# Late input products and the second short convolution placed around the first gathers, output products in quarters, row sums one slot at a time

## The reference, cut to what matters

```
z = rmsnorm(x) @ w_in                       # 19 column blocks of 128: groups A, B, C, D
A: conv31(glu) -> layernorm -> silu         # "conformer"
B: RWKV-7 time mixing, chunks of 64 tokens
C: gate_b * conv3(gate_c * hc)              # "short convolution"
D: trailing means over 2/4/8/16 positions
x = x + concat[A, B, C, D] @ w_out
q = rmsnorm(x) @ wq;  scores against 2 x 128 keys per head (8 heads)
top 16 of 16 x 16 sums -> 16 experts per token and head, gates = softmax
out = sum over experts of gate * gelu(u_e . x) * v_e;   x = x + out;  rmsnorm
```

## Time and profile before

| | us |
|---|---|
| median of 3 runs | 1668.51 |
| lowest, highest | 1665.66, 1673.72 |
| the profiled execution | 1671.36 |
| its span (first to last instruction) | 1669.6 |
| PE, DVE, ACT, POOL busy | 1220.8, 1236.3, 709.3, 916.7 |
| mean granted TensorE clock | 0.842 |
| DMA: bytes moved, mean rate | 605.42 MB, 363 GB/s |
| of it the gathers (queue 0) | 545.29 MB |

### The profile page before, as it was taken

How to read it: one execution, slowest core, us unless ns; L and a number is a source line. 1 busy time by engine, 2 the same in 40 slices (tenths; PEclk the granted TensorE clock), 3 DMA queues, 4 the chain that set the end, 5 groups by cost and what they waited for, 6 DMA issues and landing times.

```text
span 1669.6 us, 19415 instructions
## 1 busy us (share of the span) xinstructions
PE 1220.8 (73%) x5360; PEld 615.6 (37%) x5360; DVE 1236.3 (74%) x2935; ACT 709.3 (42%) x2021; POOL 916.7 (55%) x1135
## 2 busy tenths in 40 slices
PE   8998898766676877677886767675766676767564
PEld 6887756322233544332332323232322232323110
DVE  3878767788878887677778777777667776767775
ACT  3322223555454444344455654443444443434444
POOL 0364012557565766454566655565665576656662
PEclk9999999888797998788998778787878877767777
DMA  7321468999999999999999999999999999999996
GB/s 217 115 89 51 98 217 290 420 417 378 417 419 396 415 417 396 416 415 416 353 418 419 417 419 417 418 418 418 410 406 418 412 409 414 417 404 407 420 412 280
DMA packets 109308, 605.42 MB, mean 363 GB/s; under 512 B 22905, under 2 KB 25337, under 8 KB 42641
## 3 DMA queue, kind: packets, MB, share of 16 engines
q0 software_dynamic: 74880, 545.29, 79.8%
q1 hardware_dynamic: 34304, 58.89, 10.8%
q10 hardware_dynamic: 16, 0.02, 0.0%
HBM read 600.97 MB, written 3.19 MB: 362 GB/s over the span
## 4 chain that ended last, share of the span: by engine, by line
DMA 37%; PE 27%; DVE 16%; POOL 6%; issue 6%; ACT 4%; DVEq 3%; POOLq 0%; SPq 0%
DMA arena<-in_uv,arena 35%; PE ps L1011 11%; DVE arena L1979 8%; PE ps L612 5%; POOL arena L2233 4%; DVEq L1414 3%; PE ps L962 3%; DVE arena L1417 3%; POOL arena L2232 2%; PE ps L684 2%; DVE arena L1423 2%; PE ps L981 1%; ACT arena L1344 1%; PE ps L663 1%; ACT arena L1340 1%
## 5 line engine op out<-in xcount | busy, mean ns | idle before, releaser
L1011 PE MATMUL ps<-arena 128*64 128x512 f32 x2048 | 659.5, 779 | 368.5 <-ACT arena L1344 367.2
L1979 DVE CUSTOM_DVE_ANT_0 arena<-arena 128x1024 f32<-128x1024 f32 x520 | 640.8, 1234 | 292.6 <-DMA arena<-in_uv,arena 270.7
L2233 POOL DMA_INDIRECT arena<-in_uv,arena x520 | 617.8, 1188 | 87.2 <-POOL arena L2232 17.3
L2232 POOL TENSOR_TENSOR arena<-arena 1x1 f32<-1x1 f32 x520 | 216.7, 417 | 501.0 <-PE ps L1011 412.2
L1011 PEld LDWEIGHTS ps<-arena 128*64 128x64 f32 x2048 | 151.0, 164 | 754.3 <-ACT arena L1344 521.1
L1338 ACT ACTIVATE arena<-arena 128x1 f32<-128x1 f32 x520 | 105.1, 202 | 699.4 <-DVE arena L1979 697.1
L1344 ACT ACTIVATE arena<-arena 128x64 f32<-128x64 f32 (+1 forms) x520 | 181.4, 349 | 16.9
L1340 ACT ACTIVATE arena<-arena 128x1 f32<-128x1 f32 x520 | 153.2, 295 | 16.9
L1417 DVE TENSOR_TENSOR arena<-arena 128x512 f32<-128x512 f32 (+9 forms) x312 | 134.6, 432 | 21.6 <-ACT arena L1096 7.4
L612 PE MATMUL ps<-arena 128*128 128x264 f32 (+1 forms) x608 | 141.2, 386 | 0.3 <-DVE arena L1417 0.3
L962 PEld LDWEIGHTS ps<-arena 128*128 128x128 f32 x1024 | 126.9, 205 | 38.4 <-issue 37.3
...
## 6 DMA issues: line engine op xcount, KB each, us to landing
arena<-in_win SPq DMA_DIRECT2D x38, 512.0 KB, 3.4
...
arena<-in_wout SPq DMA_DIRECT2D x24, 512.0 KB, 4.9
arena<-in_uv,arena POOLq DMA_INDIRECT x520
arena<-in_xp SPq DMA_DIRECT2D x4, 512.0 KB, 6.6
out_yp<-arena SPq DMA_DIRECT2D x4, 512.0 KB
arena<-in_wqk SPq DMA_DIRECT2D x15, 128.0 KB
...
```

The source lines that it names most:

```text
L1011: last = mm(ps[64 * q:64 * q + 64, b + c, :], diag[:, (s + q) % 8, :], ring[:, SLOT_OF[TOPK * u + s + q], D + 512 * c:D + 512 * c + 512], ...
L1979: v.tensor_tensor_reduce(out=here, in0=here, in1=row, scale=1.0, scalar=0.0, op0=MUL, op1=ADD, accum_out=hsel[:, u % 2, s:s + 1]).then_inc ...
L2232: pool.tensor_tensor(carrier[:, 1:2], carrier[:, 0:1], carrier[:, 0:1], ALU.add).then_inc(S["carried"], 1)
L2233: pool.indirect_dma_start(out=ring[:, SLOT_OF[k], :], out_offset=None, in_=a["uv"][:, :], in_offset=bass.IndirectOffsetOnAxis(ap=idx[:, t, ...
```

## The change

- `SLOT_OF`, `FREE`, `FRESH`: slots 0 to 6 take seven free buffers, slots 7 to 13 reuse them, slot 14 takes the eighth and is the one that waits for all z copies. The weight ring moves below the band 1 input; slot 5 now waits until the weight ring has been used up.
- z blocks 31 to 37 leave the weight ring: they load into two buffers `zlate` from SP's `late_weights`, and PE runs one after the seventh tile 1 output block's product, one after `turned(1, ...)`, and one after each of the first five pairs of slots of unit 0. ACT copies them at the places shown. SP issues `late_weights(2)` to `(6)` before the first `next_keys`.
- `sums` handles one slot: the two column groups now hold the two halves of v, the two PSUM banks the even and the odd slot. `add_unit` adds four quarters of 64 x 512 in place of one 128 x 1024.
- `project_out` does four of eight blocks per call, at four ticks in place of two.
- Group C of band 1 moves from POOL (`short(1)`) to DVE (`short_second`), and DVE's taps, `conf_center`, `conf_scale`, `conf_swish` and the steps of `choose(1, ...)` are placed anew; the first keys are loaded three weight blocks earlier.

```
@@ -114,9 +114,9 @@
 RING = 8
-SLOT_OF = [0, 1, 2, 3, 4, 0, 1, 2, 3] + [(5, 6, 7, 4, 0, 1, 2, 3)[k % 8] for k in range(8 * 65)]
-FREE = (0, 1, 2, 3, 4, 9, 10, 11)
-FRESH = 9
+SLOT_OF = 2 * list(range(7)) + [(7, 0, 1, 2, 3, 4, 5, 6)[k % 8] for k in range(8 * 65)]
+FREE = (0, 1, 2, 3, 4, 5, 6, 14)
+FRESH = 14
@@ -136,7 +136,7 @@
...
 ZFRONT = 31
-Z_HIGH = 35
+Z_HIGH = 33
@@ -153,8 +153,7 @@
     return [("z", j) for j in range(lo, hi)]
-BLOCKS = z_blocks(0, ZFRONT) + out_blocks(0, 0, 2) + z_blocks(ZFRONT, ZFRONT + 1) + out_blocks(0, 2, 6) + z_blocks(ZFRONT + 1, ZFRONT + 2) \
-    + out_blocks(0, 6, 8) + out_blocks(1, 0, 5) + z_blocks(ZFRONT + 2, len(ZORDER))
+BLOCKS = z_blocks(0, ZFRONT) + out_blocks(0, 0, 8) + out_blocks(1, 0, 5)
@@ -295,9 +294,9 @@
...
         o_h = o_r + 3344 + 256
-        o_hb = o_ring + RING * ROW - 3 * KT * 128 - KT * GT
-        o_w = o_hb + KT * GT
-        assert o_w + 3 * KT * 128 == o_up and o_h + KT * GA <= o_hb and o_hb >= o_ring + 5 * ROW
+        o_hb = o_ring + RING * ROW - KT * GT
+        o_w = o_hb - 3 * KT * 128
+        assert o_h + KT * GA <= o_w and o_hb == o_ring + 7 * ROW and o_w >= o_ring + 5 * ROW
@@ -519,20 +521,29 @@
...
                 weights(n)
-                k = n - n_out - 8
+                k = n - n_out - 5
...
                     sp_.dma_start(wqk[:, 2048:2304], a["wqk"][0][:, 2048:2304]).then_inc(d_k12, 16)
-                elif k == 5:
-                    sp_.wait_ge(S["short_done"], 2)
-                    for i, j in enumerate(ASIDE):
-                        sp_.dma_start(w_aside[i], a["wout"][:, OUT_ORDER[j], :]).then_inc(d_aside, 16)
+            sp_.wait_ge(S["short_done"], 2)
+            for i, j in enumerate(ASIDE):
+                sp_.dma_start(w_aside[i], a["wout"][:, OUT_ORDER[j], :]).then_inc(d_aside, 16)
+
+            def late_weights(i):
+                if i >= 2:
+                    sp_.wait_ge(S["z_done"], ZFRONT + i - 1)
+                sp_.dma_start(zlate[i % 2].rearrange("p a b -> p (a b)"), a["win"][ZORDER[ZFRONT + i][0]]).then_inc(d_late[i % 2], 16)
+
             sp_.wait_ge(S["tails_done"], 3)
+            for i in range(2):
+                late_weights(i)
...
             sp_.dma_start(lora_b, a["lora"][:, :]).then_inc(d_lorab, 16)
+            for i in range(2, len(ZORDER) - ZFRONT):
+                late_weights(i)
             def next_keys(n):
@@ -601,15 +612,20 @@
...
                     i, g = ZORDER[j]
-                    n = BLOCK_OF[("z", j)]
                     lo, hi = BANDS[g]
-                    pe.wait_ge(d_w[n % 3], 16 * (n // 3 + 1))
+                    if j < ZFRONT:
+                        n = BLOCK_OF[("z", j)]
+                        pe.wait_ge(d_w[n % 3], 16 * (n // 3 + 1))
+                        w = wring[:, n % 3]
+                    else:
+                        pe.wait_ge(d_late[(j - ZFRONT) % 2], 16 * ((j - ZFRONT) // 2 + 1))
+                        w = zlate[(j - ZFRONT) % 2]
...
                     for k in range(KT):
-                        last = mm(ps[:, z_bank(j), 0:hi - lo], wring[:, n % 3, k, :], hT[g][:, k, :], start=(k == 0), stop=(k == KT - 1))
+                        last = mm(ps[:, z_bank(j), 0:hi - lo], w[:, k, :], hT[g][:, k, :], start=(k == 0), stop=(k == KT - 1))
@@ -657,11 +673,11 @@
...
                     last.then_inc(S["block_used" if j < KT - 1 else "out_mm"], 1)
-            def project_out(t, nh):
-                n, (_, y) = width(t), Y_ROWS[t]
-                for j in range(KT):
-                    last = mm(ps[0:n, 5 + nh, :], y[:, OUT_ORDER[j], :], w_blocks[j][:, 512 * nh:512 * nh + 512], start=(j == 0), stop=(j == KT - 1))
-                if nh:
+            def project_out(t, nh, part):
+                y = Y_ROWS[t][1]
+                for j in range(4 * part, 4 * part + 4):
+                    last = mm(ps[:, 5 + nh, :], y[:, OUT_ORDER[j], :], w_blocks[j][:, 512 * nh:512 * nh + 512], start=(j == 0), stop=(j == KT - 1))
+                if nh and part:
@@ -844,23 +860,22 @@
...
                 tiles = (2, 3, TILES)
-                def project(k, nh):
+                def project(k, nh, part):
                     t = tiles[k]
-                    if not nh:
+                    if not nh and not part:
...
                     if t < TILES:
-                        project_out(t, nh)
-                    else:
+                        project_out(t, nh, part)
+                    elif part:
...
                 for k in range(3):
-                    yield C_OUT + 7 * k
-                    project(k, 0)
-                    yield C_OUT + 7 * k + 4
-                    project(k, 1)
+                    for piece in range(4):
+                        yield C_OUT + 7 * k + (0, 2, 4, 5)[piece]
+                        project(k, piece // 2, piece % 2)
@@ -936,16 +951,13 @@
...
             first_out(0, 0, 2)
-            zcol()
...
             first_out(0, 2, 6)
-            zcol()
...
             first_out(1, 0, 1)
-            conf_mean(1)
@@ -1005,33 +1017,33 @@
             def sums(u, s):
                 b = 2 * (u % 2)
-                pe.wait_ge(S["diag_done"], TOPK * u + s + 2)
+                k = TOPK * u + s
+                pe.wait_ge(S["diag_done"], k + 1)
                 for c in range(2):
-                    for q in range(2):
-                        last = mm(ps[64 * q:64 * q + 64, b + c, :], diag[:, (s + q) % 8, :],
-                                  ring[:, SLOT_OF[TOPK * u + s + q], D + 512 * c:D + 512 * c + 512],
-                                  start=(s == 0 and u in FIRST_OF), stop=(s == TOPK - 2 and u in LAST_OF))
-                        if c:
-                            last.then_inc(S["slot_used"], 1)
-                for q in range(2):
-                    if u + LEAD < NU:
-                        prepare(u + LEAD, s + q)
-                    later.until(pace(TOPK * u + s + q + PE_AHEAD))
+                    last = mm(ps[64 * c:64 * c + 64, b + s % 2, :], diag[:, s % 8, :], ring[:, SLOT_OF[k], D + 512 * c:D + 512 * c + 512],
+                              start=(s < 2 and u in FIRST_OF), stop=(s >= TOPK - 2 and u in LAST_OF))
+                last.then_inc(S["slot_used"], 1)
+                if u + LEAD < NU:
+                    prepare(u + LEAD, s)
+                later.until(pace(k + PE_AHEAD))
             query(0)
+            score(0)
+            first_out(1, 1, 2)
+            conf_mean(1)
+            first_out(1, 2, 8)
+            zcol()
             conf_variance(1)
-            score(0)
-            first_out(1, 1, 8)
-            zcol(3)
...
             turned(1, 1)
+            zcol()
...
             pe.wait_ge(S["z_copied"], Z_HIGH)
-            sums(0, 0)
-            zcol()
-            sums(0, 2)
-            zcol()
+            for s in range(0, 10, 2):
+                sums(0, s)
+                sums(0, s + 1)
+                zcol()
...
             def unit(u):
@@ -1051,7 +1063,7 @@
...
                     return
-                for s in range(4 if u == 0 else 0, TOPK, 2):
+                for s in range(10 if u == 0 else 0, TOPK):
@@ -1286,9 +1298,7 @@
...
                 first.until(C_CH + 6 * c + 4)
-            zc()
             first.finish()
-            zc()
@@ -1325,7 +1335,6 @@
...
             queries(0)
-            conf_root(1)
@@ -1344,23 +1353,21 @@
...
                   scale=wgt[:, b, s:s + 1]).then_inc(S["diag_done"], 1)
-            zc()
             second_squares(1)
-            zc()
...
             zc()
+            conf_root(1)
...
             weigh(0, 1)
+            zc()
...
             weigh(0, 3)
+            zc()
...
             zc()
-            weigh(0, 4)
-            zc()
-            assert zn[0] == len(ZORDER)
@@ -1368,10 +1375,12 @@
...
                 ended = [tt for tt in range(TILES) if LAST_OF[tt] == u - 1]
-                for s in range(5 if u == 0 else 0, slots):
+                for s in range(4 if u == 0 else 0, slots):
...
                     weigh(u, s)
-                    if k == 5:
+                    if k in (5, 7, 9):
+                        zc()
+                    if k == 7:
@@ -1510,6 +1519,9 @@
...
                     dve.wait_ge(S["tails_done"], 3)
+                    dve.wait_ge(S["xpair_done"], 2)
+                    dve.wait_ge(S["out_mm"], 2)
+                    dve.wait_ge(S["z_copied"], len(ZORDER))
@@ -1770,6 +1780,20 @@
...
                 lk(last.then_inc(S["conf_out"], 1))
+            def short_second():
+
+                sw = col("sw", 0, 2 * SK).rearrange("p (a b) -> p a b", b=SK)
+                dve.wait_ge(S["short_done"], 1)
+                dve.wait_ge(S["z_copied"], ZCOUNT[(18, 1)])
+                dst = yb[:, 4:6, 0:GT]
+                lk(tt(qpad[:, :, SK - 1 + GT:], zc8[:, :, GA:NT], zh8[:, :, GA:NT], MUL))
+                for k in range(SK):
+                    for cc in range(2):
+                        o, i, w = dst[:, cc], qpad[:, cc, GT + k:GT + k + GT], sw[:, cc, k:k + 1]
```

(33 more changed lines are left out.)

7 lines of the change are left out of this document (4 added, 3 removed).

## The result

The kernel after takes 1694.68 us (median; 1690.73 to 1695.77), 1.0143 times the kernel before, with a 95% interval of 1.0121 to 1.0165. That is 20 to 28 us slower. The forecast was 1669 us and its range ended at 1684, so the forecast was wrong and the range too short. The profiled execution of after is its fastest, 1690.73 us with a span of 1688.9; against the profiled one of before (1671.36, span 1669.6) that is +19.4 us. The medians lie further apart, because the profiled execution of before was 2.9 us slower than its median and that of after 4.0 us faster; no trace shows where these 7 us lie.

A forecast was written before the change was run, and what follows sets the result against it. The prediction took DMA queue filling, 520 gathers and dry time as the bound. 1671.4 + 14 (wait for z37) - 14 (stream) = 1671.4, on the median 1669 us; own range 1658 to 1681, range leaving out 2 in 10: 1646 to 1684.

The forecast's parts named there:

- The bound: Whole kernel: time is filling the DMA queue, plus 520 gathers, plus every microsecond the queue runs dry.
- First gather: Start: first gather leaves at 250.5, not 257.5, 7 us sooner; bounds 0 and 9.
- first gather no sooner: Rival for the start: weights set the pace from further back, +7, 1676 us; chance 5 %.
- Second scores: Start, after the second query: scores ready at 269, where they are taken at 278.8 before.
- The wait for z37: Start: slot 14 waits for z37's copy, leaves near 322.5, lands at 328.3, not 314.2: +14 us, bounds +9 and +20.
- By then one gather is in flight: Reason given in the wait for z37 for second keys landing after 5 us, from a range of 4.9 to 10.5.
- The stream: Behind the start: buffers released sooner and shorter output products win back dry time, -14 us, bounds -4 and -22.5.
- every gather goes out 2 to 3 us sooner: Stream: single-slot sums return an even slot's buffer 3.4 us sooner, an odd slot's 2.2, so gathers leave earlier.
- The cost of the new form: Row sums by single slot: 0.12 us more PE time per pair, 31 us in all, beside the DMA.
- All other bytes of the start are the same in both: Start: apart from the wait for slot 14, the bytes moved were taken as unchanged.
- the hole: Start: DMA engines idle for over 20 us before slot 14's gather, costing +14 us, bounds +9 and +20.
- the hole stays and the stream does not pay it: Rival, behind 330: late buffers come from other PE work or lower clock; return only 4, 1678.5 us; chance 25 %.

The follow-up runs named there:

- s3: Kernel before with only the stream part: sums one slot at a time, `add_unit` in quarters, output products in quarters, old start; ratio 0.9964.
- s1: Kernel before with row sums slot by slot and the row added in quarters, output products still in halves; ratio 0.9973.
- b3: Kernel after with z products and second keys earlier, eighth ring row at slot 21, last two z blocks behind sums 5 and 7, copies behind softmax; ratio 0.9989.

## Why the prediction was wrong

**The bound** held. The time is the time at which the queue is filled, plus the stream, plus dry time. The table shows it: the last dot follows the dot of slot 24 by 1320 to 1321 us with pairs and halves, 1317.7 with pairs and quarters, and 1312.5 to 1317.6 in the nine kernels with release by slot.

**First gather**, predicted 250.5, came at 252.45: 5.0 us sooner than before, where 7 were forecast. The step was right, 2 us too large. On DVE, the reciprocals and the residual:

```profile
214.76 3.58 DVE L1680 RECIPROCAL arena<-arena 128x256 f32<-128x256 f32 x2 [0.86 <-ACT arena L1233]
...
227.69 1.22 DVE L1426 TENSOR_TENSOR arena<-arena,ps 128x1024 f32<-128x1024 f32 x1 [2.62 <-PE ps L672]
```

The reciprocals end at 218.3, 6.4 us sooner than before, and the short convolution's second half fits in before the residual, which waits 2.6 us for PE all the same: it cost nothing. The residual begins at 227.7 and not near 225, which is where the 2 us are missing. The rival "first gather no sooner" is out.

**Second scores**, predicted 269: taken by DVE at 271.12, 7.7 us sooner than before. Right, once the 2 us of the first gather are carried over.

**The wait for z37** is the step that failed, in its size and not in its mechanism. Every link is there in the order written down. Predicted were 322.5 for slot 14's issue, 14 us of hole, bounds 9 to 20. It left at 329.2, and the dots stand 24 us behind those of before (slot 19 at 349.4 and 325.5). The 10 us by which its dot is later than the predicted 328.3 (338.2) are:
- 3.7 us at z35: it ended at 293.2 and not 289.5. 1.8 of it is carried: z35 began at 287.75 and not at 286, since the first gather and the second scores came 2 us after their forecasts. The other 1.9 is its length: it ran 5.41 us, in part at the lower clock, where a warm block, 3.5, had been set down. PE had just waited twice (1.4 and 2.2 us). The prediction had a cold PE for query(2) but not for this block.
- 2.2 us at the keys: 8.7 us from the first issue to the start of query(2), where 6.5 had been taken; 2.7 of it is SP issuing four transfers, and 6.0 is from the last issue to the query. "By then one gather is in flight" was not the whole of it: the last z weight block, issued at 293.2 just ahead of the keys, and the row of slot 13, issued at 295.9, shared the DMA engines with them, and these stayed full until 302 (the row of 296 to 302 below). The landing lies between the short end (5) and the long one (10.5).
- 0.8 us net from there to slot 14's issue: the sums 8 and 9 took 3.68, at the lower clock, and not 2.0; other links were a little shorter than set down.
- 3.3 us behind the issue: the dot came 9.1 us after it, not 5.8. It did not wait for its row. DVE, with its wait for z37 over, did dots 11 to 13, waited 2.2 us for scores and did work of the mixer first; the first dot that waits for its row again is that of slot 17. The prediction took the landing time of one late gather for the restart of the whole stream.

These are lined up so that the carried delays aren't counted twice; they sum to 10.0. The granted clock (the number ahead of the DMA share) in after, in a stretch of the second query, of z35, of the wait for the keys, of the third query, of the sums 8 and 9, and of z37:

```profile
266.00:270.00 4.00, 3.75 (x33) 3.54 (x31) 1.03 (x3) 0.60 (x2) 0.00 (x0) 1.00 1.01 421
...
288.00:293.00 5.00, 5.00 (x16) 3.84 (x15) 3.19 (x7) 0.00 (x0) 1.05 (x2) 0.66 0.97 338
296.00:302.00 6.00, 0.00 (x0) 0.00 (x0) 0.00 (x0) 0.00 (x0) 0.90 (x1) 0.71 1.01 348
302.00:307.00 5.00, 4.73 (x29) 4.73 (x30) 0.00 (x0) 0.00 (x0) 0.00 (x0) 0.67 0.12 49
...
320.00:323.00 3.00, 3.00 (x8) 0.59 (x8) 1.87 (x5) 0.85 (x3) 0.00 (x0) 0.50 0.01 3
323.50:328.00 4.50, 4.50 (x18) 3.75 (x16) 0.00 (x0) 0.00 (x0) 0.00 (x0) 0.74 0.00 0
```

1.00 is 2.4 GHz and 0.50 is 1.2 GHz; a mean between them is a stretch with some of both. z35, the third query, the sums 8 and 9 and z37 all run in part or in whole at 1.2 GHz, each behind waits of PE; single sums behind waits of 1.3 to 2.2 us still took 1.08 us. The upper bound of 20 took only late keys. Late keys and a lower clock were not independent chances: in these rows the stretches at the lower clock all follow the waits that lengthen the chain.

**The stream**, predicted -14, is -5.9 by the table, and 0.36% or 6.0 us in s3. By parts: 800 to 840 as predicted (6 of 6.7 us; 6.5 came), 300 to 500 as predicted (2.5 of 3.8; 3.5 came in 340 to 400), and 500 to 800 not at all: 4.5 of 5.7 were taken, and the rate went from 410 to 409. The end, set at 0, cost 3.7: the last 30 us lose 7.9 where they lost 4.2. The first and second part less this end are 6.3 us, beside the 5.9 of the table. In 500 to 800 the prediction read a rate of 410 at a DMA share of 1.01 as late buffers, although it refused that very reading for 1200 to 1640 two lines further. The share said the same in both. From the issue of a gather to the dot that waited for its row it takes 11.0 to 14.2 us for slots 26 to 30 before, and 14.3 to 17.6 in s1: a gather that goes out sooner only stands longer in a queue that is not empty. So the step that failed is "every gather goes out 2 to 3 us sooner" as a price: it happens, and it was worth time only where the share was under 1.

**The cost of the new form** was set at 0.12 us per pair, 31 us of PE in all. The groups of the row sums in the two pages, before and after:

```profile
L1011 PE MATMUL ps<-arena 128*64 128x512 f32 x2048 | 659.5, 779 | 368.5 <-ACT arena L1344 367.2
```

```profile
L1023 PE MATMUL ps<-arena 128*64 128x512 f32 x2048 | 676.8, 769 | 292.1 <-ACT arena L1353 289.4
```

17 us more, and the mean of one instruction is no longer than before. What the Trainium skill says of the drain at a change of the tiling mode (TensorEngine Tiling (Array Packing), "Key Properties") shows as no separate cost here: the single slot takes 1.08 us, a pair of them 1.94 where both are ready, and whatever a drain costs lies within the 0.2 us between two singles and a pair.

**Bytes.** "All other bytes of the start are the same in both" is wrong: five z weight blocks are issued behind the first gather where two were. In after this does not show, since the queue is dry from 302 to 329 anyway; in b3, without that hole, it is some 3 us.

**The sum.** The two failed terms, +10 on the hole and +8 on the stream, are 18 of the 19.3 us between forecast and profile. The rival that had the right sign had half of it: "the hole stays and the stream does not pay it" gave a return of 4 (5.5 to 6 came) but kept the hole at 14. No case combined a hole at its upper bound with a small return. Neither error alone would have left the range (1678.5 and 1676.5 on the median); both together did. That combination, +20 - 4, is 1684.5 on the median, where the range ended; the hole was longer than even that bound.
